# Mixing the two softmaxes of a differential attention before the turn, so that V is multiplied once

## The reference, cut to what matters

```
def diff_group(q, k, v, lq1, lk1, lq2, lk2, norm_g, lam_init):
    ...
    o1 = block_attention(q1, k1, v, bias, scale)
    o2 = block_attention(q2, k2, v, bias, scale)
    lam = (exp(sum(lq1 * lk1)) - exp(sum(lq2 * lk2)) + lam_init)
    o = o1 - lam * o2
    o = rmsnorm(o, norm_g) * (1.0 - lam_init)
```

## Time and profile before

| | us |
|---|---|
| median of 3 runs (2664.87 to 2671.57) | 2667.25 |
| the profiled execution, its own time | 2663.74 |
| its span, first to last instruction | 2662.3 |
| PE busy in the span | 2594.2 (97%) |
| DVE busy | 1161.6 (44%) |
| ACT busy | 908.8 (34%) |

### The profile page before, as it was taken

The page is one execution under the profiler, slowest core; times in us unless marked ns, Lnnn a source line. Parts: engine busy times, 40 slices in busy tenths (PEclk is TensorE's granted clock), DMA queues, the critical chain, the costliest instruction groups (busy, mean ns, idle before and its releaser), DMA issues.

```text
span 2662.3 us, 33423 instructions
## 1 busy us (share of the span) xinstructions
PE 2594.2 (97%) x13512; PEld 1811.1 (68%) x13516; DVE 1161.6 (44%) x2176; ACT 908.8 (34%) x1747; POOL 355.6 (13%) x162
## 2 busy tenths in 40 slices
PE   7999999999999999999989999999999999999999
PEld 6875444444777444445477778888888777888887
DVE  3543223322786233223355343562555534465264
ACT  4431111111483111111164454442345445443233
POOL 2200000000340000000030011221222101123212
PEclk9999999999999999999999999999999999999999
DMA  6129999999324999999922012322132111223212
GB/s 215 66 100 421 419 421 421 421 421 420 110 95 170 421 421 421 421 421 421 380 92 80 32 64 78 97 95 95 64 115 83 48 48 53 76 95 111 85 63 83
DMA packets 139036, 543.30 MB, mean 204 GB/s; under 512 B 18816, under 2 KB 30336, under 8 KB 89728
## 3 DMA queue, kind: packets, MB, share of 16 engines
q1 hardware_dynamic: 129264, 536.94, 51.6%
q10 hardware_dynamic: 9616, 4.18, 0.6%
HBM read 538.99 MB, written 2.10 MB: 203 GB/s over the span
## 4 chain that ended last, share of the span: by engine, by line
PE 91%; DVE 4%; ACT 2%; issue 1%; POOL 0%; DMA 0%; ACTq 0%; POOLq 0%; DVEq 0%
PE ps L615 23%; PE ps L1413 17%; PE ps L617 14%; PE ps L1435 8%; PE ps L1388 5%; PE ps L637 5%; PE ps L549 3%; PE ps L1450 3%; PE ps L2003 2%; PE ps L1451 2%; PE ps L1976 2%; PE ps L550 1%; PE ps L1995 1%; PE ps L467 1%; DVE w L279 1%
## 5 line engine op out<-in xcount | busy, mean ns | idle before, releaser
L615 PE MATMUL ps<-w,w 128*128 128x512 f32 x2976 | 678.9, 390 | 2.6 <-POOL w L279 2.6
L615 PEld LDWEIGHTS ps<-w,w 128*128 128x128 f32 x2976 | 558.0, 188 | 119.5 <-POOL w L279 3.4
L279 POOL TENSOR_TENSOR w<-w,w 128x1024 fp32r<-128x1024 f32 (+2 forms) x136 | 331.5, 2447 | 2175.3 <-ACT w L271 2171.0
L1413 PE MATMUL ps<-w,w 128*64 128x512 f32 x2048 | 451.6, 594 | 1.8 <-issue 1.8
L617 PE MATMUL ps<-w,w 128*128 128x512 f32 (+1 forms) x1872 | 408.1, 379 | 3.3 <-DVE w L535 3.0
L271 ACT ACTIVATE w<-w 128x1024 fp32r<-128x1024 f32 (+2 forms) x260 | 252.9, 1001 | 410.9 <-PE ps L615 178.4
L617 PEld LDWEIGHTS ps<-w,w 128*128 128x128 f32 x1872 | 337.9, 188 | 69.8 <-issue 4.8
L279 DVE TENSOR_TENSOR w<-w,w 128x1024 fp32r<-128x1024 f32 (+2 forms) x124 | 210.9, 1708 | 378.6 <-ACT w L271 376.1
L1413 PEld LDWEIGHTS ps<-w,w 128*64 128x64 f32 x2048 | 146.0, 137 | 285.6 <-issue 285.6
L1674 DVE TENSOR_TENSOR X<-ps,X 128x512 f32<-128x512 f32 x256 | 162.3, 682 | 181.7 <-PE ps L1451 180.7
L1435 PE MATMUL ps<-w,w 128*64 128x512 f32 x1024 | 226.8, 595 | 0.8 <-ACT w L1502 0.8
(11 more groups left out here) (253 smaller groups left out, 2339.7 us busy)
## 6 DMA issues: line engine op xcount, KB each, us to landing
w<-in_moe_w_gate SPq DMA_DIRECT2D x128, 1024.0 KB, 15.0
w<-in_moe_w_up SPq DMA_DIRECT2D x128, 1024.0 KB, 17.2
w<-in_moe_w_down SPq DMA_DIRECT2D x128, 1024.0 KB, 14.4
w<-in_w_up SPq DMA_DIRECT2D x40, 1024.0 KB, 5.1
w<-in_w_down SPq DMA_DIRECT2D x20, 1024.0 KB, 5.1
w<-in_w_in SPq DMA_DIRECT2D x16, 1024.0 KB, 5.2
w<-in_ab_w_in SPq DMA_DIRECT2D x10, 1024.0 KB, 5.1
w<-in_c_w_in SPq DMA_DIRECT2D x8, 1024.0 KB, 6.9
```

What stands on the lines that cost most here:

```text
L279: up(self.wlo[self.low[s][0]], lane.e.tensor_tensor(lo, raw, hi.bitcast(F32), ALU.subtract))
L615: ins = pe.matmul(bank[:, :], wp[:, k, P * o:P * o + P], ap(k0 + k), start=first, stop=stop)
L1413: ins = pe.matmul(bank[64 * e:64 * e + 64, :], XG[p % 3][:, 4 * u + k, 64 * e:64 * e + 64], w[e][:, k, :], start=(u == 0 and k == 0), stop ...
```

## The change

The two softmaxes of a diff pair are mixed ahead of the turn. VectorE's turn part takes the reciprocals as before, multiplies the second sum's reciprocal by the first sum and by -lam (`share`, one number a row), and then, in place, PB[diff0] = PB[diff1] * share + PB[diff0] over n*128 columns. TensorE's turn part waits for this (`mixed`) where before it waited for the exponentials (`bsc.free`), and it transposes, copies and multiplies by V one buffer for each diff pair. The output is scaled by the reciprocal of the first sum. Since a diff pair now has one turn and other pairs have two, `turn_of` counts turns apart from jobs: semaphore values and the index of PTB go by it. O1B and its two passes are gone, and the reciprocals have places of their own in AT.

```
         def tensor_turn(m, two):
-            for m, job in zip((m, m + 1), two):
-                PE.wait_ge(bsc.free, m + 1)
+            for m, job in turned_jobs(m, two):
+                if job[1] == "diff0":
+                    PE.wait_ge(mixed, (m - M_DIFF) // 2 + 1)
+                else:
+                    PE.wait_ge(bsc.free, m + 1)
                 bank = banks.take(bpt)
                 for j in range(job[0] + 1):
                     ins = pe.transpose(bank[:, P * j:P * j + P], PB[m % 4][:, P * j:P * j + P], ident)
                 up(bpt.full, ins)

         def tensor_values(m, two):
-            for m, (qc, _, _, _, _, vals, dv) in zip((m, m + 1), two):
-                PE.wait_ge(bpt.free, m + 1)
+            for m, (qc, _, _, _, _, vals, dv) in turned_jobs(m, two):
+                n = turn_of(m)
+                PE.wait_ge(bpt.free, n + 1)
...
         def scalar_turn(m, two):
-            for m, job in zip((m, m + 1), two):
+            for m, job in turned_jobs(m, two):
...
         def vector_turn(m, two):
             V.wait_ge(bsc.free, m + 2)
-            sm = AT[:, 8 + m % 8:10 + m % 8]
-            up(rc, dve.reciprocal(sm, sm))
+            n, i0 = P * (two[0][0] + 1), m % 8
+            up(rc, dve.reciprocal(AT[:, 16 + i0:18 + i0], AT[:, 8 + i0:10 + i0]))
+            if two[0][1] == "diff0":
+                V.wait_ge(nlam, 1)
+                V.wait_ge(rc, m // 2 + 1)
+                share = AT[:, 24 + i0:25 + i0]
+                vstep(dve.tensor_scalar(share, AT[:, 8 + i0:9 + i0], AT[:, 17 + i0:18 + i0], LS[:, 3:4], ALU.mult, ALU.mult))
+                up(mixed, dve.scalar_tensor_tensor(PB[m % 4][:, 0:n], PB[(m + 1) % 4][:, 0:n], share, PB[m % 4][:, 0:n],
+                                                   ALU.mult, ALU.add))

         def vector_values(m, two):
...
-                if kind == "diff0":
-                    up(bo.free, dve.tensor_scalar(O1B[:, qc, :], bank[:, 0:dv], sm, None, ALU.mult))
-                elif kind == "diff1":
-                    V.wait_ge(nlam, 1)
-                    V.wait_ge(bo.free, m)
-                    vstep(dve.tensor_tensor(sm, sm, LS[:, 3:4], ALU.mult))
-                    o = O[:, qc, 256 + P * h:384 + P * h]
-                    up(bo.free, dve.scalar_tensor_tensor(o, bank[:, 0:dv], sm, O1B[:, qc, :], ALU.mult, ALU.add))
...
+                c0 = 256 + P * h if kind == "diff0" else (768 if kind == "mla" else 0) + 64 * h
+                up(bo.free, dve.tensor_scalar(O[:, qc, c0:c0 + dv], bank[:, 0:dv], AT[:, 16 + m % 8:17 + m % 8], None, ALU.mult))
```

More of the change, by code:

```diff
@@ L333, in program @@
     dnB = sb("dnB", [P, 2, 128])
-    AT = sb("AT", [P, 16])
+    AT = sb("AT", [P, 32])
     sb_cum = sb("sb_cum", [P, 80])
@@ L1859, in program @@
     bsc, bpt, bo = handoff("scores"), handoff("turned"), handoff("values")
-    lam_in, lam_out, nlam, ckv, q1k1, mx, rc, o_done, cum, cum_parts = (
-        sig(n) for n in ("lam_in", "lam_out", "nlam", "ckv", "q1k1", "max", "recip", "o_done", "cum", "cum_parts"))
+    lam_in, lam_out, nlam, ckv, q1k1, mx, rc, mixed, o_done, cum, cum_parts = (
+        sig(n) for n in ("lam_in", "lam_out", "nlam", "ckv", "q1k1", "max", "recip", "mixed", "o_done", "cum", "cum_parts"))
     OUT_ORDER = (1, 0)
@@ L1901, in attention @@
         DV = at_(16384, 4, 512)
-        O1B = at_(18432, 4, 128)
         SQ = at_(18944, 16, 128, dt=BF16)
@@ L1937, in attention, with turn_of, turned_jobs @@
         M_DIFF, M_FOX = len(mla_jobs), len(mla_jobs) + len(diff_jobs)
+        N_TURNS = M_FOX - len(diff_jobs) // 2 + len(fox_jobs)
+        def turn_of(m):
+            if m < M_DIFF:
+                return m
+            return M_DIFF + (m - M_DIFF) // 2 if m < M_FOX else m - len(diff_jobs) // 2
+        def turned_jobs(m, two):
+            return [(m + k, job) for k, job in enumerate(two) if job[1] != "diff1"]
         def pipeline(jobs, m0, engine, at_step, steps):
@@ L1998, in tensor_values @@
         def tensor_values(m, two):
-            for m, (qc, _, _, _, _, vals, dv) in zip((m, m + 1), two):
-                PE.wait_ge(bpt.free, m + 1)
+            for m, (qc, _, _, _, _, vals, dv) in turned_jobs(m, two):
+                n = turn_of(m)
+                PE.wait_ge(bpt.free, n + 1)
                 bank = banks.take(bo)
                 for j in range(qc + 1):
-                    ins = pe.matmul(bank[:, 0:dv], PTB[m % 4][:, P * j:P * j + P], vals(j), start=(j == 0), stop=(j == qc))
+                    ins = pe.matmul(bank[:, 0:dv], PTB[n % 4][:, P * j:P * j + P], vals(j), start=(j == 0), stop=(j == qc))
                 up(bo.full, ins)
@@ L2071, in rest @@
                     rest_of_third(engine)
-                    PE.wait_ge(bo.free, M_FOX + len(fox_jobs))
+                    PE.wait_ge(bo.free, N_TURNS)
                     tensor_o_features(FEATURES_OUT[6:])
@@ L2088, in scalar_scores @@
                 if m > 3:
-                    S.wait_ge(bpt.full, m - 3)
+                    S.wait_ge(bpt.full, turn_of(m - 4) + 1)
                 S.wait_ge(mx, m + 1)
@@ L2094, in scalar_turn @@
         def scalar_turn(m, two):
-            for m, job in zip((m, m + 1), two):
+            for m, job in turned_jobs(m, two):
                 n = P * (job[0] + 1)
                 bank = bpt.next(S)
-                if m > 3:
-                    S.wait_ge(bo.full, m - 3)
-                up(bpt.free, act.activation(PTB[m % 4][:, 0:n], bank[:, 0:n], ACT.Copy))
+                turn = turn_of(m)
+                if turn > 3:
+                    S.wait_ge(bo.full, turn - 3)
+                up(bpt.free, act.activation(PTB[turn % 4][:, 0:n], bank[:, 0:n], ACT.Copy))
         def scalar_values(m, two):
@@ L2156, in scalar @@
                       lambda: scalar_product(("fqk", i), fqk_evacuate))
-            S.wait_ge(bo.free, M_FOX)
+            S.wait_ge(bo.free, turn_of(M_FOX))
             for c in range(NT):
@@ L2187, in vector_turn @@
             V.wait_ge(bsc.free, m + 2)
-            sm = AT[:, 8 + m % 8:10 + m % 8]
-            up(rc, dve.reciprocal(sm, sm))
+            n, i0 = P * (two[0][0] + 1), m % 8
[7 more added lines that the diff above has]
+                                                   ALU.mult, ALU.add))
         def vector_values(m, two):
-            for m, (qc, kind, h, _, _, _, dv) in zip((m, m + 1), two):
-                sm = AT[:, 8 + m % 8:9 + m % 8]
+            for m, (qc, kind, h, _, _, _, dv) in turned_jobs(m, two):
                 bank = bo.next(V)
                 V.wait_ge(rc, m // 2 + 1)
-                if kind == "diff0":
-                    up(bo.free, dve.tensor_scalar(O1B[:, qc, :], bank[:, 0:dv], sm, None, ALU.mult))
-                elif kind == "diff1":
-                    V.wait_ge(nlam, 1)
-                    V.wait_ge(bo.free, m)
-                    vstep(dve.tensor_tensor(sm, sm, LS[:, 3:4], ALU.mult))
-                    o = O[:, qc, 256 + P * h:384 + P * h]
-                    up(bo.free, dve.scalar_tensor_tensor(o, bank[:, 0:dv], sm, O1B[:, qc, :], ALU.mult, ALU.add))
-                else:
-                    c0 = (768 if kind == "mla" else 0) + 64 * h
-                    up(bo.free, dve.tensor_scalar(O[:, qc, c0:c0 + 64], bank[:, 0:dv], sm, None, ALU.mult))
+                c0 = 256 + P * h if kind == "diff0" else (768 if kind == "mla" else 0) + 64 * h
+                up(bo.free, dve.tensor_scalar(O[:, qc, c0:c0 + dv], bank[:, 0:dv], AT[:, 16 + m % 8:17 + m % 8], None, ALU.mult))
         def vector_o_features(ks):
```

## The result

| | before | after |
|---|---|---|
| median, us | 2668.28 (4 runs, 2664.87 to 2671.57) | 2724.47 (4 runs, 2717.16 to 2728.25) |
| ratio | | 1.0204, 95% interval 1.0184 to 1.0224 |
| span of the profiled execution | 2662.3 | 2724.5 |
| transposes (L1995, now L2008), records | 320 | 240 |
| mean granted clock | 0.996 | 0.972 |

The changed kernel is slower by 56 us or 2.0%. TensorE has less work, 240 fewer matmul records (80 of transposes, 160 of values), and VectorE is busy for 11 us more only.

A forecast was written before the change was run, and what follows sets the result against it. TensorE alone was taken to set the pace. To 2667.25 us before, the loop net of gains adds 20 and the clock 24, giving 2711 us; range from 2680 to 2735, and 2 more for a mixing at 0.75.

The forecast's parts named there:

- The likeliest of the cases: Steps 10 to 22: TensorE and VectorE wait in a loop and the clock falls for half the loops; 2711 us, chance 0.65.
- the high end: All loops at 1.2 GHz and a longer recovery in the projection, 2735 us, and 2 more for a mixing at 0.75.
- Two of the signs named ahead: Steps 10 to 22 of each layer taking 49 to 60 us; TensorE's transposes waiting 1.5 to 2.5 us, 13 times a layer.
- Removed work: Diff pairs' transposes and value matmuls halved: about 80 fewer transposes, 160 fewer records, 29 us of TensorE's work over two layers.
- The loop: Steps 10 to 22: turn, scores, maxima, output, reciprocals, share, mixing in sequence; period 15.1 us against 11.34, stretch 49.3 for 37.11.
- The mixing itself: VectorE's mixing pass in the loop, taken on a straight line: 0.35, 0.48, 0.61, 0.75 us for n = 1 to 4.
- Step 23 and the tail: Stretches after the loops that keep a gain: step 23 shorter by 1.1 us and the tail by 1.0, each layer.
- The clock: Half of the 13 loops at 1.2 GHz plus 3.4 us of the next projection at half speed: +12 us a layer, +24 in two.
- The price of a period at 1.2 GHz: Steps 10 to 22 with the clock down: each loop 1.6 us longer than at 2.4 GHz.
- case B: Steps 10 to 22: the loop as priced, but the clock at 2.4 GHz throughout; 2687 us, chance 0.24.
- C: Wait ahead of the transposes: VectorE keeps ahead, the engines overlap and the busier binds; -27 us, 2640 us, chance 0.06.

The follow-up runs named there:

- fill: The changed kernel with five matmuls without use (512 columns) behind the values of each step 10 to 22; 2690.6 us, ratio 1.0086 to the kernel before.
- scores_first: The changed kernel with TensorE doing the scores of pair p ahead of the turn of pair p-2 in steps 11 to 23; 2655.47 us, ratio 0.9952.
- output_between: scores_first with VectorE's output pass, in steps 12 to 23, for the pair one step older and between mixing and maxima; 2650.51 us, ratio 0.9942.
- work_only: The kernel before with share and the mixing pass added on VectorE, into a spare buffer nobody reads or waits for; 2668.4 us, ratio 1.0007.
- narrow_mix: fill with the mixing pass cut to the first 128 columns of each pair; 2689.45 us, ratio 1.0088 to the kernel before.
- fill_two: fill with two matmuls without use in each gap in place of five; 2694.71 us, ratio 1.0104 to the kernel before.

## Why the prediction was right, and where its sizes were off

- **Direction and mechanism.** Slower, by a closed loop of TensorE and VectorE in which neither overlaps, and a clock that falls on top. All of it is in the trace: 28 waits for L2212 (13 and the one of the tail, in each layer), 1.5 us each on average (41.7 / 28), and the clock at 0.60 and 0.54. The likeliest of the cases came, and 2724 lies in the range 2680 to 2737, but 13 us above the 2711 forecast: it lies nearer to the high end, which has every loop at 1.2 GHz (2735 us), than to the forecast, and both sums were too low, the loop's by 4 us and the clock's by 11. Two of the signs named ahead were missed: the 13 steps took 65.3 and 68.4 us where 49 to 60 stood, and the waits were 1.34 to 1.64 us long where 1.5 to 2.5 stood.
- **Removed work.** 80 fewer transposes and 160 fewer records of values, as forecast; together they are the 240 by which TensorE's count fell.
- **The loop.** 13 loops at 2.4 GHz were priced at 49.3 us and took 51.61 (fill); a period 15.1, measured 15.78. Two terms were short and one was long. `share` (L2211) holds the mixing back by 0.31 us (1494.91 to 1495.22), not by the 0.195 that I took from L2201, a simpler operation on the same shape: 0.46 a period. And transposes that start after a wait take longer than those in a stream, 0.37 and 0.59 us for two and four where I had 0.25 and 0.50, some 0.4 a period over the four widths. Against them, TensorE starts 0.06 us behind the end of the mixing (1495.57 to 1495.63 above), not 0.15, 0.36 a period. What is left of the difference of 0.7, some 0.2, is not attributed. The mixing itself was priced right: 0.35, 0.48, 0.62, 0.75 us.
- **Step 23 and the tail.** -1.1 and -1.0 forecast. In fill, step 23 takes 1.78 us (53.39 - 51.61), so -1.06; the tail is 1.35 shorter. So the loop's net cost is 51.61 - 37.11 - 1.06 - 1.35 = 12.1 us a layer and 24 in two (20 forecast). fill is 24 us over the kernel before.
- **The clock** is the term that was mis-sized. I took half of the loops at 1.2 GHz and 24 us in two layers. After its second fall in the first layer the clock didn't come back before the projection, and in the second layer it fell once and didn't come back before the projection either: the 13 steps are 13.7 and 16.8 us longer than in fill, step 23 1.4 each, the projections 1.0 each, 35 us in all. By 1.5 us a loop, that is some 9 and 11 of the 13 loops. The price of a period at 1.2 GHz came out, 15.1 + 4 x 1.6 = 21.5 us for 21.7 measured, but by two errors that offset each other: the period at 2.4 GHz is 0.7 longer, and the clock adds 1.5 us a loop, not 1.6. Wrong was that the loop at 1.2 GHz, busy for some 70%, would be enough to bring 2.4 GHz back half of the time. The rows had no such stretch. They had one in which TensorE worked without a gap until the clock rose, and that was the row to take. Even that is no rule: the gapless work of an n=4 loop brought the clock back once, at 1494 us, and not in the same loops at 1508 and 1530 us, nor in the second layer.
- **The rule of the Trainium skill** ("TensorE: Matmul & The Clock Gate", section "HAM oscillation — how this bites in real kernels"), taken as one about long idle pieces, would have given case B, 2687 us. The trace decides against that reading: no gap in these steps is over 1.7 us, and the clock fell.
- **Rivals.** B is what fill is, 2690.6 for the 2687 forecast. C did not occur in the order as written; scores_first shows that its condition was named right: once the mixing has other TensorE work to lie under, the change gains, though 11 us and not 27, since turn, values, output and mixing still form a loop. The Trainium skill, "Perfetto Trace Analysis", section "Identifying the Most-Contended Engine", would have the engine with the highest occupancy relieved. The time of output_between agrees (2650.5 us), that of the changed kernel doesn't (2724.5 us): there the relief went in together with a wait.

## What to carry to other kernels

Work that is taken from a saturated engine and given to an idle one costs nothing while nobody waits for it (work_only), and its whole length where the saturated engine does (narrow_mix): write down the order of both programs and follow the wait once round, and if it closes within one step, put the work of another pair between. If the new loop leaves TensorE half idle, count its matmuls at 1.2 GHz for the whole stretch and into the next one, as it came out here; filling the gaps with matmuls of no use tells the two costs apart in one run.

## What the runs showed of the hardware

- TensorE fell from 2.4 to 1.2 GHz with no gap longer than 1.61 us: at 1501 us, behind 5 us with 2.76 us of work and waits of 1.34 and 1.61 us. In the 50 us from 1500 on it worked for 36.2 us, in pieces of at most 4.6 us, and the clock stayed at 1.2 GHz but for the first microsecond. It rose within the first 5 us of the projection, in which TensorE had no gap. The windows of both:

```profile
1500.00:1550.00 50.00, 36.23 (x146) 21.69 (x146) 19.31 (x56) 15.53 (x50) 0.00 (x0) 0.51 0.00 1
...
1550.00:1555.00 5.00, 5.00 (x19) 4.07 (x19) 0.35 (x1) 0.00 (x0) 0.00 (x0) 0.77 0.00 0
```

- The same loop of fill_two ran at 1.2 GHz once and at 2.4 GHz in the periods behind it, with waits of up to 1.51 us.
- A VectorE operation on one number a row with two scalar operands from memory (L2211) takes 0.27 us, one with two tensor operands (L2201) 0.16 us.
- The mixing pass follows a straight line in its width, all operands in SBUF: 352, 484, 618 and 752 ns for 128 to 512 columns, 1.04 ns a column.
